# High and low latents side by side in one 512-column product for the query and mix panels

## What is computed

```
ul = (xl * (1 + sc1_l) + sh1_l) @ w_in        # combined input projection, latents
uc = (xc * (1 + sc1_c) + sh1_c) @ w_in        # context
ya = head_rms_norm(gated recurrence, both directions) * silu(gl)   # branch A
yb = grouped centred means, mixed, scaled                          # branch B
yc = windowed attention with a sink, rotary positions              # branch C
x1 = layer_norm(ALPHA * xl + g1 * (sum_j sigmoid(gate_j) * (y_j @ w_branch_j)) @ w_out)
out = layer_norm(ALPHA * x1 + g2 * square(relu(mod(x1) @ w1)) @ w2)
```

## Time and profile before

| | us |
|---|---|
| median of 3 runs | 1930.51 |
| lowest and highest run | 1928.32, 1932.26 |
| the profiled execution | 1933.53 |
| its span (first to last instruction) | 1931.7 |
| busy: TensorE | 1870.1 |
| busy: VectorE | 1283.3 |
| busy: ScalarE | 810.2 |
| busy: GpSimd | 277.5 |

### The profile page before, as it was taken

How to read it: one execution, slowest core, us unless ns; L and a number is a source line. 1 busy time by engine, 2 the same in 40 slices (tenths; PEclk the granted TensorE clock), 3 DMA queues, 4 the chain that set the end, 5 groups by cost and what they waited for, 6 DMA issues and landing times.

```text
span 1931.7 us, 23993 instructions
## 1 busy us (share of the span) xinstructions
PE 1870.1 (97%) x9784; PEld 1562.1 (81%) x9784; DVE 1283.3 (66%) x1454; ACT 810.2 (42%) x971; POOL 277.5 (14%) x165
## 2 busy tenths in 40 slices
PE   5999999999999999999999998999999999999997
PEld 1568987899999887878888887888888888888875
DVE  1236767785868766486676666786676567557786
ACT  1132234464555554444444434543344344434432
POOL 0000000004838253000010100120012001100100
PEclk8999999999999999999999999999999999999999
DMA  9956765554333454385676754565665565656642
GB/s 400 421 223 249 274 218 174 175 175 153 129 134 110 140 209 163 131 288 213 244 273 233 273 198 173 218 237 183 243 246 203 196 218 218 218 196 223 235 168 94
DMA packets 59598, 408.90 MB, mean 212 GB/s; under 512 B 6368, under 2 KB 9056, under 8 KB 10848
## 3 DMA queue, kind: packets, MB, share of 16 engines
q1 hardware_dynamic: 55008, 395.34, 56.0%
q10 hardware_dynamic: 4480, 12.02, 1.7%
HBM read 405.24 MB, written 2.10 MB: 211 GB/s over the span
## 4 chain that ended last, share of the span: by engine, by line
PE 87%; DVE 7%; DMA 2%; issue 1%; POOL 1%; DVEq 1%; ACT 1%; SPq 0%; ACTq 0%
PE main L1423 14%; PE main L1424 14%; PE main L1425 14%; PE side L1400 6%; PE main L1400 6%; PE main L1360 4%; PE main L1362 4%; PE main L1361 4%; PE side L1402 3%; PE main L1402 3%; DVE asum L940 2%; DMA raw<-in_w_ada 2%; PE main L1474 2%; DVE wlo L919 2%; PE main L1476 2%; PE main L1475 2%
## 5 line engine op out<-in xcount | busy, mean ns | idle before, releaser
L919 DVE TENSOR_TENSOR wlo<-raw,whi 128x1024 fp32r<-128x1024 f32 x548 | 703.8, 1311 | 356.4 <-ACT whi L457 355.7
L457 ACT CAST whi<-raw 128x1024 fp32r<-128x1024 f32 x548 | 570.3, 1052 | 745.0 <-PE main L1425 406.6
L1360 PE MATMUL main<-hCL,whi 128*128 128x256 f32 (+1 forms) x768 | 249.0, 324 | 8.0 <-ACT cq L623 4.4
L1362 PE MATMUL main<-hCL,wlo 128*128 128x256 f32 (+1 forms) x768 | 246.0, 320 | 0.0
L1361 PE MATMUL main<-hCL,whi 128*128 128x256 f32 (+1 forms) x768 | 245.8, 320 | 0.0
L940 DVE SCALAR_TENSOR_TENSOR asum<-raw,sm,asum 128x512 f32<-128x512 f32 x240 | 221.8, 924 | 19.5 <-issue 0.4
L1423 PE MATMUL main<-whi,hid 128*128 128x512 f32 x496 | 194.9, 393 | 2.8 <-DVE wlo L919 2.8
L1424 PE MATMUL main<-wlo,hid 128*128 128x512 f32 x496 | 193.1, 389 | 0.0
L1425 PE MATMUL main<-whi,hid 128*128 128x512 f32 x496 | 193.1, 389 | 0.0
L1400 PE MATMUL main<-h,whi 128*128 128x512 f32 x512 | 183.8, 403 | 4.8 <-DVE h L1255 2.5
L1400 PE MATMUL side<-h,whi 128*128 128x512 f32 x512 | 181.3, 399 | 0.0
(11 more groups left out here) (246 smaller groups left out, 2861.6 us busy)
## 6 DMA issues: line engine op xcount, KB each, us to landing
raw<-in_w_f SPq DMA_DIRECT2D x128, 1024.0 KB, 4.9
raw<-in_w_in SPq DMA_DIRECT2D x104, 1024.0 KB, 4.9
raw<-in_w_ada SPq DMA_DIRECT2D x96, 1024.0 KB, 5.5
raw<-in_w_br SPq DMA_DIRECT2D x24, 1024.0 KB, 4.9
raw<-in_w_out SPq DMA_DIRECT2D x16, 1024.0 KB, 4.8
xin<-in_xT SPq DMA_DIRECT2D x4, 1024.0 KB, 15.4
raw<-in_w_ck SPq DMA_DIRECT2D x4, 512.0 KB, 12.9
raw<-in_w_cv SPq DMA_DIRECT2D x2, 1024.0 KB, 4.9
```

Source lines behind the costliest of these rows:

```text
L457: nc.scalar.copy(half_at(q)[0], slots[slot][:, 2 * h:2 * h + 2]).then_inc(hi_made, 1)
L919: TT(half_at(q)[1], slots[slot][:, 2 * h:2 * h + 2], half_at(q)[0].bitcast(F32), ALU.subtract).then_inc(lo_made, 1)
L1360: mm(out, w_hi, x_hi, start=start, stop=False)
L1362: return mm(out, w_lo, x_hi, start=False, stop=stop)
```

## The change

Queries and mix use `wide` with `hL` in place of `features`: per k-tile and bank one product of 512 columns (2 x 256 latents, high and low) and one of 256. Every bank is now emptied by ScalarE's copy of the first half and then VectorE's add of the second, in place; VectorE signals that the bank is free. The output gate's Tanh and product now read the sum in SBUF, with `cq` as room for the Tanh.

```diff
-    pn.add("query", 0, 4, four, "A")
-    pn.add("query", 4, 4, four, "V")
+    for n in range(2):
+        pn.add("query", 4 * n, 4, four, "V")
     for i in range(2):
-        for n, who in enumerate("VAV"):
-            pn.add("mix", 12 * i + 4 * n, 4, four, who)
+        for n in range(3):
+            pn.add("mix", 12 * i + 4 * n, 4, four, "V")
...
+            def first_half(name, first, out):
+
+                for b in range(4):
+                    blk(name, first, b)
+                    nc.scalar.copy(out[:, b], main[:, b, 0:T]).then_inc(low_in, 1)
...
-                if k == 3:
-                    for b in range(4):
-                        blk("query", 0, b)
-                        nc.scalar.copy(q_t[:, b], main[:, b, 0:T]).then_inc(freed["A"], 1)
+                if k % 4 == 3:
+                    first_half("query", k - 3, q_t[:, k - 3:k + 1])
...
+                    if k % 4 == 3:
+                        own = slice(4 * i, 4 * i + 4)
+                        first_half("mix", 12 * i + k - 3, (ya, cq, xb)[k // 4][:, own])
                     if k == 3:
                         for b in range(4):
-                            blk("mix", 12 * i, b)
-                            A(ya[:, i * 4 + b], main[:, b, 0:T], ACT.Tanh, scale=0.5).then_inc(gs_sig, 1)
-                    if k == 7:
-                        for b in range(4):
-                            blk("mix", 12 * i + 4, b)
-                            nc.scalar.copy(cq[:, i * 4 + b], main[:, b, 0:T]).then_inc(freed["A"], 1)
+                            act.wait_ge(freed["V"], PN.own["mix", 12 * i] + b + 1)
+                            A(cq[:, 4 * i + b], ya[:, 4 * i + b], ACT.Tanh, scale=0.5).then_inc(gs_sig, 1)
...
+            def second_half(out, done):
+                for b in range(4):
+                    dve.wait_ge(low_in, done + b + 1)
+                    TT(out[:, b], out[:, b], main[:, b, T:2 * T], ALU.add).then_inc(freed["V"], 1)
+
             for k in range(8):
                 split_after("query", k)
                 if k < 4:
                     gate_block(3, k, True)
-            for b in range(4):
-                blk("query", 4, b)
-                nc.vector.tensor_copy(q_t[:, 4 + b], main[:, b, 0:T]).then_inc(freed["V"], 1)
+                if k % 4 == 3:
+                    second_half(q_t[:, k - 3:k + 1], k - 3)
...
+                    if k % 4 == 3:
+                        own = slice(4 * i, 4 * i + 4)
+                        second_half((ya, cq, xb)[k // 4][:, own], 8 + 12 * i + k - 3)
                     if k == 3:
                         for b in range(4):
-                            blk("mix", 12 * i, b)
                             dve.wait_ge(gs_sig, i * 4 + b + 1)
-                            STT(ya[:, i * 4 + b], ya[:, i * 4 + b], 1.0, main[:, b, 0:T], ALU.add,
-                                ALU.mult).then_inc(freed["V"], 1)
-                    if k == 11:
-                        for b in range(4):
-                            blk("mix", 12 * i + 8, b)
-                            nc.vector.tensor_copy(xb[:, i * 4 + b], main[:, b, 0:T]).then_inc(freed["V"], 1)
+                            STT(ya[:, i * 4 + b], cq[:, i * 4 + b], 1.0, ya[:, i * 4 + b], ALU.add, ALU.mult)
...
-                                mm(ps[:, b], whi[:, par, j, own], h2[:, kt].rearrange("p v t -> p (v t)"),
+                                mm(ps[:, b].rearrange("p (v t) -> p v t", v=2), whi[:, par, j, own], x[:, kt],
                                    start=kt == 0, stop=kt == 15, skip_group_check=True)
-                                last = mm(ps[:, b, 0:T], wlo[:, par, j, own], h2[:, kt, 0], start=False,
+                                last = mm(ps[:, b, 0:T], wlo[:, par, j, own], x[:, kt, 0], start=False,
                                           stop=kt == 15, skip_group_check=True)
...
-            features("query", 0, hCL, C, C + T, between=query)
-            features("query", 4, hCL, C, C + T, between=lambda k: query(k + 4))
+            wide("query", 0, main, hL, between=query)
+            wide("query", 4, main, hL, between=lambda k: query(k + 4))
...
-                    features("mix", 12 * i + 4 * n, hCL, C, C + T, between=lambda k, n=n: beside(4 * n + k))
+                    wide("mix", 12 * i + 4 * n, main, hL, between=lambda k, n=n: beside(4 * n + k))
```

More of the change, by code:

```diff
@@ L379, in build @@
          at_v, at_sc, at_max, at_exp, at_norm, at_tr, at_cp, at_o, at_y, y_hi, y_lo, pool_diff, pool_ps, pool_y, m_done,
-         m_tr, m_hi, m_lo, ax_in, var_in, rs_out, nm_out, h2_tr, h2_hi, h2_lo, x1_done, hid_in, hid_pos, hid_hi, hid_lo, y_out, cleared) = (
+         m_tr, m_hi, m_lo, ax_in, var_in, rs_out, nm_out, h2_tr, low_in, h2_hi, h2_lo, x1_done, hid_in, hid_pos, hid_hi, hid_lo, y_out, cleared) = (
             sem(x) for x in (
@@ L385, in build @@
             "at_v at_sc at_max at_exp at_norm at_tr at_cp at_o at_y y_hi y_lo pool_diff pool_ps pool_y m_done "
-            "m_tr m_hi m_lo ax_in var_in rs_out nm_out h2_tr h2_hi h2_lo x1_done hid_in hid_pos hid_hi hid_lo y_out cleared").split())
+            "m_tr m_hi m_lo ax_in var_in rs_out nm_out h2_tr low_in h2_hi h2_lo x1_done hid_in hid_pos hid_hi hid_lo y_out cleared").split())
         n_done = [sem("n_done_first"), sem("n_done_second")]
@@ L1385, in features, with wide @@
                     between(n)
-            def wide(name, first, ps, ready=None, between=lambda k: None):
+            def wide(name, first, ps, x=h2, ready=None, between=lambda k: None):
                 for n in range(4):
```

## The result

The changed kernel takes 1947.0 us (median of 6 runs, 1944.3 to 1951.3) against 1930.1 us (6 runs): slower, ratio 1.0090, 95% interval 1.0077 to 1.0103. The forecast was slower too, but by 4.1 us, and 1947 lies outside its range.

A forecast was written before the change was run, and what follows sets the result against it. TensorE, busy 1870.1 of 1931.7 us, was taken as the bound. Products -3.7 after swallowed gains, query wait +3.5, clock +1.5, panel 7 +1.3, gates +1.5: together +4.1 us, 1934.6 for the median; range 1930 to 1940.

The forecast's parts named there:

- Products: Query and mix panels: pairs instead of triples win 0.12 or 0.20 us per panel, 5.9 us over 32 panels.
- 2.2 us of waits: Part of the products' gain swallowed by waits: 0.6 us at the query switch and 1.6 in the mix.
- count of panels that follow another directly: Six of the 32 query and mix panels, winning 0.12 us each; the 26 others win 0.20.
- Query switch: First query group to second: adds stand behind head 3's gate block; TensorE waits some 4.1 us, costing +3.5 us.
- The term for the clock: After the query wait: at least one fall to half clock, +1.5 us, bounds 0 and 3.
- Mix panel 3, "cost 0": Bank switch after mix panel 3: the wait stays, new work behind it is covered; cost 0, without cover 1.7 us.
- Rival A: VectorE's queue decides in more places, gating products at panel 3 delay splits: +7.1 to +11.1 us; chance 0.18.
- Mix panel 7: Bank switch after mix panel 7: the add waits for VectorE's masked copy, +0.63 us twice, +1.3 us.
- Mix to gates, "+1.5": Second pass into gates: bank copies before the swap delay casts, inverse root, outputs and split; net 1.0 to 2.1 us.
- the 0.25 us at panel 1: Gates: later casts for panel 1 cost 0.25 us ahead of the split for panel 2.
- The upper bound of 3: Upper bound of the mix-to-gates cost, 3 us, with a fall of the clock.

The follow-up runs named there:

- rotation_later: The changed kernel with GpSimd's first rotation held until VectorE has made the head outputs of the second pass; ratio 1.0114 to the kernel before.
- wait_kept_busy_15: The changed kernel with 15 small float32 products, results unused, on TensorE behind query panel 3; ratio 1.0072 to the kernel before.
- swap_first: The changed kernel with ScalarE's four swap copies ahead of the last four bank copies in the second mix pass; ratio 1.0047 to the kernel before.
- q_adds_first: The changed kernel with VectorE's four adds of the first query group ahead of the gate block of head 3; ratio 1.0053 to the kernel before.

## Why the forecast was right in its sign and wrong in its size

**Products.** Right: 5.63 us for a panel after small products. By itself the pair is worth it to TensorE; beside the same order with three products the program sees 0.9 us of it, for longer waits take up 2.8 us and the fall of the clock behind one of them 1.5. I had allowed for 2.2 us of waits. (The prediction's count of panels that follow another directly leaves out query panel 4; that is under 0.1 us.)

**Query switch.** Right: the wait was forecast at 4.1 and is 4.07 us. The term for the clock was 1.5, with 3 as its upper bound; it measured 2.4 to 2.5 (8.11 against 5.63 to 5.74 us). In rotation_later, whose program is the same up to there, the same wait of 4.07 us was followed by a panel of 7.25, 1.6 us more; so the forecast 1.5 lies as near to what can follow this wait as the 2.5 does, and the wait alone doesn't decide which comes.

**Mix panel 3, "cost 0".** Failed in the second pass: 2.90 us against 1.82 before, and a half-clock stretch behind it (7.22 us for the panel, against the forecast 5.63): 2.7 us. There the splits ran beside GpSimd's arguments from the start: the four took 7.4 us from 583.20 on, against 6.4 before, and the exponential that holds the copies waits for them. That this was due to those splits was only read from the timeline. The fall is in part chance: the same wait of 2.90 us in wait_kept_busy_15 had none behind it. Rival A, with a chance of 0.18, named this place, but for both passes, for another reason (the gating products), and with a total of 7.1 to 11.1 us. Of its reason something is there: the four gating products took 2.96 us in the first pass and 2.19 in the second, where 1.7 was forecast, but behind the wait and not ahead of it.

**Mix panel 7.** 3.16 and 3.21 us; named as 2.9 to 3.5, with VectorE, and VectorE's adds start at 525.93, right behind the masked copy of 524.68. Right. A wait of 0.4 us for a split ahead of panel 7 in the first pass was not foreseen.

**Mix to gates, "+1.5".** This is the step that failed most: 5.9 us. The chain was right (bank copies, swap, casts, inverse root, outputs, split), and so were the start of the swap and the 0.25 us at panel 1 (0.29). I left the outputs their duration of before, though, 1.67 us, and gave only the split behind them a slowed rate. Moving the swap moved GpSimd's rotation too, onto the outputs, which it stretched to 4.61. The wait became 3.95 us where 0.41 was; rotation_later shows that without the collision it is 0.5. A fall of the clock followed (granted clock 0.66 from 679 to 684). The upper bound of 3 came from treating collision and clock as alternatives; both happened. In swap_first the part from the first gates product to the first with a branch's input takes 24.0 us, against 29.8 in the changed kernel and 23.8 before.

**What stays open.** In the profiled executions 14.2 us are lost, in the medians 16.9. 1.5 us of the 14.2 lie outside the stretch, where the programs are alike; the profiled run of before was 3.5 us above its median, that of the change 0.8.

## What to carry to other kernels

When an eviction moves to another engine, or to two, write down for each bank switch what stands ahead of it in each engine's program, and where the work that it pushes back lands; a late start is cheap until it falls together with the work of an engine that slows it. First try the order of the old kernel: here moving the evictions ahead of work that waits for others won 7.5 us, more than the shorter products could. A wait of TensorE must be priced with the half clock that may follow it, and a single execution says little about a difference of 1 or 2 us, since such a fall comes in one and not in the next.

## What the runs showed of the hardware

- The same wait is followed by half clock or not. After mix panel 3 of the first pass it was 2.12 us in two kernels. In q_adds_first the clock fell (the busy times of the stretch behind it, granted clock 0.81):

```profile
487.00:496.00 9.00, 8.42 (x43) 7.42 (x44) 8.90 (x14) 7.67 (x12) 3.21 (x3) 0.81 0.06 13
```

In rotation_later it stayed (1.00):

```profile
488.00:497.00 9.00, 8.02 (x52) 7.26 (x53) 8.49 (x13) 8.02 (x14) 4.00 (x5) 1.00 0.05 14
```

The Trainium skill ("TensorE: Matmul & The Clock Gate", the part on the clock gate) says that the check's phase runs free of the program; these runs agree.
- Over the bank switches of all runs: behind 1.7 to 1.8 us (4 waits) the clock never fell, behind 2.0 to 2.3 in 6 of 13, behind 2.7 to 2.9 in 4 of 7, behind 3.1 to 3.2 in all 14. A fall made the next panel 1.3 to 1.6 us longer; one of the 14 cost 2.9 (a panel of 8.49 in wait_kept_busy_15). Behind the four waits of 4.1 us the panel took 7.25 to 8.37 us, 1.6 to 2.7 more.
- A float32 product of 128 columns shows as two matmul records: 30 products gave 60 and took 6.6 us.
- Four VectorE operations of 128x256 with two inputs in SBUF took 1.67 us alone and 4.61 beside GpSimd, and GpSimd's own multiplication of 128x1024 took 4.46 us beside VectorE's splits (rotation_later) against 2.39 before. Four of the adds, which have one input in the bank, took 1.40 us beside GpSimd (the changed kernel at 525.93), no more than in the MLP.
